# Expert activations and their weighing in one program, with the first weighing group prepared during the last expert steps

## What is computed

```python
best, ci = lax.top_k(cand, 16)            # 16 of 256 candidate pairs, per token and head (8 heads)
e = i1[ci // 16] * 128 + i2[ci % 16]      # expert numbers, 128 picks a token
g = softmax(best)
hid = einsum('td,tkd->tk', xn, u[e])      # one dot product with row e of u
act = gelu(hid) * g
out = einsum('tk,tkd->td', act, v[e])     # weighted sum of rows e of v
```

## Time and profile before

| | us |
|---|---|
| median of three runs (3413.38 to 3416.85) | 3415.7 |
| the profiled execution, its own time | 3419.49 |
| its span in the trace | 3417.7 |
| TensorE busy in the span | 3182.4 (93%) |
| VectorE, ScalarE, GpSimd busy | 2177.6, 1223.9, 1682.6 |

### The profile page before, as it was taken

One profiled execution on the slowest core, in us unless ns is written; L12 is line 12 of the kernel. 1 busy time (PEld: TensorE's weight loads), 2 busy tenths in 40 slices (PEclk: granted clock), 3 DMA queues, 4 the chain that ended last, 5 costly groups with the idle time before them and its releaser, 6 DMA issues. The chain is left out here.

```text
span 3417.7 us, 45006 instructions
## 1 busy us (share of the span) xinstructions
PE 3182.4 (93%) x17090; PEld 2878.5 (84%) x17090; DVE 2177.6 (64%) x3550; ACT 1223.9 (36%) x1895; POOL 1682.6 (49%) x847
## 2 busy tenths in 40 slices
PE   7989678988999999999999999994999999999998
PEld 5777578877889999999999999993888888888886
DVE  2510578824455678687878889773667666666664
ACT  3211347722112225655555656651211211212110
POOL 2411010022203565555554555675878778778783
PEclk9999789999999999999999999997999999999999
DMA  3242652141214676767676767888778788787784
GB/s 136 87 166 76 152 112 47 29 166 59 68 46 133 207 239 193 258 230 240 233 247 222 240 231 233 305 320 326 291 287 308 281 295 291 287 305 274 280 305 149
DMA packets 253406, 713.94 MB, mean 209 GB/s; under 512 B 21681, under 2 KB 79921, under 8 KB 246577
## 3 DMA queue, kind: packets, MB, share of 16 engines
q1 hardware_dynamic: 179504, 443.13, 38.1%
q0 software_dynamic: 73728, 268.47, 22.7%
HBM read 577.31 MB, written 134.22 MB: 208 GB/s over the span
## 5 line engine op out<-in xcount | busy, mean ns | idle before, releaser
L1228 DVE SCALAR_TENSOR_TENSOR found<-found,x_first 128x1024 f32<-128x1024 f32 x232 | 406.5, 1765 | 245.7 <-DMA found<-in_u,pick_u 245.0
L1299 PE MATMUL banks<-side_hi,u_hi 128*128 128x384 f32 x2048 | 533.0, 341 | 14.3 <-issue 14.3
L968 POOL TENSOR_TENSOR u_lo<-u_raw,u_hi 128x1024 fp32r<-128x1024 f32 x127 | 338.8, 2668 | 392.0 <-ACT u_hi L918 391.5
L1299 PE MATMUL banks<-side_lo,u_hi 128*128 128x384 f32 x2048 | 523.7, 336 | 0.0
L1299 PE MATMUL banks<-side_hi,u_lo 128*128 128x384 f32 x2048 | 522.7, 336 | 0.0
L2006 PE MATMUL part<-v_hi,act_hi 128*128 128x512 f32 x1536 | 475.8, 391 | 49.6 <-POOL act_lo L1929 49.6
L2006 PE MATMUL part<-v_lo,act_hi 128*128 128x512 f32 x1536 | 474.7, 390 | 0.0
L2006 PE MATMUL part<-v_hi,act_lo 128*128 128x512 f32 x1536 | 474.2, 390 | 0.0
L977 POOL DMA_INDIRECT found<-in_u,pick_u x232 | 336.6, 1451 | 196.8 <-DVE found L1228 158.8
L1945 DVE TENSOR_TENSOR acc<-acc,part 128x1024 f32<-128x1024 f32 x192 | 234.3, 1220 | 302.6 <-PE part L2006 302.3
L1897 ACT ACTIVATE v_hi<-v_raw 128x2048 fp32r<-128x2048 f32 x64 | 122.9, 1920 | 799.2 <-DMA v_raw<-in_v 614.8
(11 more groups left out here) (217 smaller groups left out, 5196.0 us busy)
## 6 DMA issues: line engine op xcount, KB each, us to landing
u_raw<-in_uT SPq DMA_DIRECT2D x128, 512.0 KB
v_raw<-in_v SPq DMA_DIRECT2D x64, 1024.0 KB
hid_d<-hid SPq DMA_DIRECT2D x128, 384.0 KB, 5.7
gate_d<-stage SPq DMA_DIRECT2D x48, 1024.0 KB
act_in<-hid_d SPq DMA_DIRECT2D x64, 768.0 KB, 7.7
gate_in<-gate_d SPq DMA_DIRECT2D x32, 1536.0 KB
w_raw<-in_w_in SPq DMA_DIRECT2D x6, 2048.0 KB, 8.2
k_hi<-k_hi_d SPq DMA_DIRECT2D x32, 256.0 KB, 8.0
```

Of the source, the lines that this page charges most:

```text
L968: pool.tensor_tensor(u_lo[s % 2][:, :, :], u_raw[:, :, :], u_hi[s % 2][:, :, :].bitcast(F), ALU.subtract).then_inc(u_lo_ok, 1)
L1228: dve.scalar_tensor_tensor(out=found[:, g], in0=found[:, g], scalar=1.0, in1=x_first[:, g], op0=ALU.mult, op1=ALU.mult, accum_out=pick_act ...
L1299: mm = pe.matmul(hid_ps[:, s % 2, half, 0:W], w[s % 2][:, ch], x[:, ch, GB * P + half * W:GB * P + (half + 1) * W], start=n == 0, stop=n = ...
```

## The change

`route`, `hidden` and `weigh` now lie in one program with no barrier between them. The semaphores are made once for all three. `weigh`'s buffers take the place of those of `hidden`, ordered so that what is free early is used early: `v_hi` and `v_lo` are `side_hi` and `side_lo`, the hidden activations of group 0 go to `act_first` and `act_in[1]`, its second pair of `v` to one of the four `found4` buffers.

During the last turn SyncE loads group 0 after step 13 (`load_first`). Group 0's gates are read for 640 of the 768 dense tokens, since the last block's come last (`EARLY_T`). VectorE multiplies after its products of step 15, ScalarE rounds the product ahead of its Gelu of step 15 and `v` behind it. TensorE goes from the last expert step to group 0's item 0. Low parts of group 0's `v` are made by VectorE (columns 0, 1, 3) and GpSimd (column 2). The other 128 tokens follow when the last gates are stored and read back (`last_gates`); item 5 waits for them.

The lags are shorter, `(6, 11)`, and the ranking of blocks 0 and 1 takes fewer slots (`near`), so that gathers begin at steps 6 and 11. In turn 0 there is one product per step and block. `late_picks` then has 6 and 11, over by step 12.

The core of the diff (indentation left out; a line that is only "..." marks what is left out):

```diff
-    LAG = (SLOTS // 2, SLOTS)
+    LAG = m.lag                     # (6, 11)
...
-            return [(g, s * LAG[g] // SLOTS) for g in range(GB) if s * LAG[g] % SLOTS == 0]
+        return [(0, s // 2)] * (s % 2 and s // 2 < LAG[0]) + [(1, s)] * (s < LAG[1])
...
+        def load_first():
+            for n in range(2):
+                sp.wait_ge(hid_out[n], 16 * blocks)
+            sp.wait_ge(stage_out[0], 16 * PARTS * (blocks - GB))
+            sp.wait_ge(stage_out[1], 16 * PARTS * (blocks - GB - 1))
+            for x, rows in ((0, m.act_first), (1, m.act_in[1])):
+                sp.dma_start(rows[:, :, :], hid_d[COLS * x:COLS * x + COLS]...).then_inc(m.a_in[x], 16)
+            sp.dma_start(m.gate_in[:, 0:EARLY_Q], gate_d[0:EARLY_Q, :, 0:2 * COLS]...).then_inc(m.g_in, 16)
+            sp.dma_start(m.v_raw[:, :, :], v_d[0:COLS]...).then_inc(m.v_in, 16)
+            for g in range(GB):
+                sp.wait_ge(late_dotted[g], LAG[g])
+            sp.dma_start(m.found4[1][:, :, :], v_d[COLS:2 * COLS]...).then_inc(m.v_in, 16)
...
+                if last and s == 13:
+                    load_first()
...
-            for n in range(PARTS):
-                store_gates(blocks - 1, PER, n)
-            for s in range(2):
-                sp.wait_ge(hid_out[s], 16 * blocks * SLOTS // 2)
-                sp.wait_ge(stage_out[s], 16 * PARTS * (blocks - GB))
...
-                    if s == (9 if phase and phase <= GB else 12) and not last:
+                if s == (7 if phase == 0 else 9 if phase <= GB else 12) and not last:
                         exponents(tb + 1)
...
+            near = quick and tb < GB
...
-                if phase == 0:
+                if phase == 0 and s == LAG[1] - 1:
                     keep_picks(1)
...
@@ weigh, TensorE: the first group @@
+        def group_first():
+            for n in range(DENSE):
+                if n < BANKS:
+                    pe.wait_ge(m.hid_ok, ALL_STEPS - 1 + n)
+                else:
+                    pe.wait_ge(added, n - BANKS + 1)
+                if n == DENSE - 1:
+                    pe.wait_ge(a_lo_ok, 1 + HALVES)
...
+                    if n == 0:
+                        pe.wait_ge(v_hi_ok, j + 1)
+                        pe.wait_ge(m.a_lo_first if x else a_lo_ok, 1)
...
@@ layer @@
-        weigh(nc, v, hid_d, gate_d, h_d, pick_v, pick_act, out)
+                weigh(nc, block, sem, m, side_hi, side_lo, v, hid_d, gate_d, h_d, pick_v, pick_act, out)
```

More of the change, by code:

```diff
@@ L427, in __init__ @@
[L427 to L436, removed]
@@ L463, in route @@
     KEYS = 2 * PEER_HEADS
[L464 to L524, removed]
@@ new lines, in route @@
+    x_in = sem("x_in3")
+    small_in = sem("small_in3")
+    first_in = [sem(f"first_in3{n}") for n in range(4)]
+    first_lo = [sem("first_lo_pool"), sem("first_lo_dve")]
+    w_in = sem("w_in3")
+    w_hi_ok = sem("w_hi_ok3")
+    w_lo_ok = sem("w_lo_ok3")
+    u_in, u_hi_ok, u_lo_ok = m.u_in, m.u_hi_ok, m.u_lo_ok
+    const_ok = sem("const_ok3")
+    pr_ok = sem("pr_ok3")
+    added = sem("h_added")
+    h_out = sem("h_out")
+    ss_ok = sem("ss_ok3")
+    var_ok = sem("var_ok3")
+    rstd_ok = sem("rstd_ok3")
@@ L775, in hidden @@
+def hidden(nc, block, sem, m, x_hi, x_lo, x_first, iota, iota16, ident, uT_d, u_d, v_d, score_d, hid_d, gate_d,
            pick_v, pick_act, blocks=TB):
@@ new lines, in _, with turn, body @@
+    @block.tensor
+    def _(pe):
+        def turn(tb):
+            pe.wait_ge(looked, LOOKS * (tb + 1))
+            for n, src in enumerate((expert[:, 0], expert[:, 1], share[:, :, :])):
+                last = pe.transpose(turn_ps[:, n], src.rearrange("p h k -> p (h k)"), ident[:, :])
+            last.then_inc(turned, 1)
+        def body(tb, phase, last):
+            for s in range(SLOTS):
+                j = tb * SLOTS + s
+                pe.wait_ge(u_lo_ok, j + 1)
+                if phase == 0 and s < 2:
+                    pe.wait_ge(m.q_ok, 2 * SLOTS)
+                if not (phase == 0 and s < 2):
+                    pe.wait_ge(hid_ok, j - 1)
+                n = 0
+                for ch in range(C):
+                    for w, x in ((u_hi, x_hi), (u_hi, x_lo), (u_lo, x_hi)):
+                        for half in range(2):
+                            mm = pe.matmul(hid_ps[:, s % 2, half, 0:W], w[s % 2][:, ch],
+                                           x[:, ch, GB * P + half * W:GB * P + (half + 1) * W],
+                                           start=n == 0, stop=n == 3 * C - 1)
+                        n += 1
+                mm.then_inc(hid_mm, 1)
+                if s == 15 and phase and not last:
+                    turn(tb + 1)
+                if phase < GB:
+                    continue
+                if not (phase == GB and s == 0):
+                    pe.wait_ge(gate_ok, j - NO_GATES)
+                pe.wait_ge(col_ok, j - NO_GATES + 1)
+                for t in range(TOK):
+                    mm = pe.matmul(gate_ps[:, t], row_hot[:, s % 2, t], col_gate[:, s % 2, t],
+                                   start=True, stop=True)
+                mm.then_inc(gate_mm, 1)
+        for tb in range(GB + 1):
+            body(tb, tb, False)
+        with pe.Fori(GB + 1, blocks - 1) as tb:
+            body(tb, GB + 1, False)
+        body(blocks - 1, GB + 1, True)
```

1887 lines of the change are left out of this document (1028 added, 859 removed), and 3 rows, old and new, of the table EXPERT_SIGNALS.

## The result

| | before | the change |
|---|---|---|
| median of four runs each, us | 3414.5 | 3434.65 (3433.87 to 3435.82) |
| ratio to before | | 1.0061, 95% interval 1.0048 to 1.0074 |
| span of the profiled execution | 3417.7 | 3432.4 |

The account below looks back on a forecast made before the run. The weighing loop was taken as bound by TensorE, the seam costing 55.8 us beyond its own work. Terms left 23.6 us, so 32.2 gained: 3415.7 - 32.2 = 3383.5 us, range 3368 to 3401.

Parts of the forecast that it names:

- The "slower" one: Rival, weighing loop: GpSimd's gathers and low parts settle behind, every group begins with a wait; 3446 us at 2 us each; chance 0.04.
- sign of being wrong: TensorE's waits from 2300 us on not adding up to 14 to 22 us, or waits standing after group 1.
- the late gates: Seam, group 0: last gates read back at 2329, the addition done by 2331.2, in time, so no wait.
- the transfers collide: Rival, seam: loads, stores and gathers share the DMA engines; gain only 18 or 15 us, 3401 us; chance 0.14.
- the lags: Expert steps: gathers beginning at steps 6 and 11 lose nothing and gain nothing, as TensorE had no gap there.
- restart: Start of group 0 at the seam: TensorE idles from 2300.4 to 2307.0, 6.6 us.
- low parts of `v` in item 0: First item of group 0: v blocks follow each 1.06 us, so the item runs through without a wait.
- item 3, the seed: Group 0: the seed's load and copy delay VectorE's second addition to 2326.8; TensorE waits 1.5 us.
- item 5, gates of group 1: Group 0: VectorE waits for group 1's gates before the addition this item needs; TensorE waits 5.9 us.
- group 1, second half: Group 1: GpSimd's low parts are done at 2357.3; TensorE waits 3.6 us from 2353.7.
- lower clock: After seam waits TensorE runs at the lower clock, costing 2.0 us each time.
- The rate of 0.39 MB per us: Seam: the speed at which the full DMA engines were taken to move loads, stores and gathers.

Follow-up runs that it names:

- e1: The change with 32 unused bytes a partition behind its small buffers, moving all buffers of the three stages 32 bytes further on; 3396.4 us, ratio 0.9937.
- e11: The kernel of e1 run again, unchanged, on the chip of e10; 3394.35 us, ratio 0.9938 to the kernel before.
- e7: The kernel of e1 with three of the four last gate stores moved behind the load of group 1's gates; 3408.5 us, ratio 0.9974.
- e8: e7 with the seam reordered: first gate store, seed and late gates ahead of most sums, second v last; 3400.3 us, ratio 0.9956.
- e10: e8 with group 1's v loaded right behind the late gates, its gates last, and ScalarE rounding v without waiting for stores; 3396.7 us, ratio 0.9952.
- e6: The kernel before with only the new lags of 6 and 11 and the earlier ranking of the first two blocks; 3406.9 us, ratio 0.9976.

## Why the prediction was wrong

**The step that failed** is the sentence "New semaphores and unrolled loop turns on SyncE cost nothing visible: under 1 us either way", at the end of its paragraph on the shorter lags. It weighs what the program gained in instructions, and leaves out that joining the programs laid all their buffers out anew. TensorE's time per matmul was taken as a constant of the loop (0.227). It was 0.2338 in the change. That cost 29.9 us in the loop, 1.0 in the 156 matmuls ahead of it (156 x 6.7 ns), 6.7 in `route` (1026.35 less 1019.69 in e1): 37.6 together, and e1 measured 38.2 for the whole. The last term is good to some 3 us: in the kernels whose `route` was fast the first Gelu stood at 1016.9 to 1019.7. None of the rivals had it. The "slower" one (GpSimd's loop settling behind) gave 3446 by another mechanism, of which there is no sign: no wait stands among the 4452 matmuls.

The prediction's own sign of being wrong showed too, apart from the placement: the waits from 2300 on were to be 14 to 22 us, and were 30.4 (29.1 in e11). The largest term behind that is the late gates, put at 0, which measured 7.8.

With the placement mended, e1 and e11 took 3396.4 and 3394.35 us. Those lie inside the range, above the forecast of 3383.5, close to the rival "the transfers collide". In part that is luck: the seam gave 17 us and not 32, and the lags, put at 0, gave 8.4 that the sum didn't have. The rival's terms don't fit one by one either, with 5 us for the seed (measured 0.6) and nothing for the late gates (7.6).

**The seam, term by term** (waits of TensorE in us; the third clock term falls behind the seam as measured here):

| term | predicted | change | e11 |
|---|---|---|---|
| restart | 6.6 | 8.2 | 8.0 |
| low parts of `v` in item 0 | 0 | 1.4 | 1.1 |
| item 3, the seed | 1.5 | 0.5 | 0.6 |
| item 4, the late gates | 0 | 7.8 | 7.6 |
| item 5, gates of group 1 | 5.9 | 6.7 | 6.1 |
| group 1, second half | 3.6 | 5.8 | 5.7 |
| lower clock | 4.0 | 5.8 | 7.5 |

The last row is what is left of the seam: 72.7 - 30.4 - 156 x 0.2338 for the change, 72.0 - 29.1 - 156 x 0.2271 for e11. Predicted were 21.6 us, measured 36.2 and 36.6: the gain is 17 us, where 32.2 stood.

- *Restart*: right in kind and near in size. VectorE's last product ended 2.3 us behind the last expert matmul (2303.02 + 1.22), where 0.5 was said; the chain has its gather at 10.59 us, where 5.1 to 8.9 had been read. The v blocks followed as foreseen.
- *The late gates* are the term of the seam that was mis-sized most. The prediction has "the rest of 0.79" MB behind the first store, which is three quarters of 1.05: four stores taken as 1.05 MB in all. Each is 1 MB. The first landed 14.5 us after its issue and the reading back took another 11.6: at 2342.78, where 2329 was said. Counted from the last expert matmul that is 40.9 us for 28.6. The first store alone landed 4.7 later than said (29.3 for 24.6), and e7 shows the part of the 3.1 MB behind it: 7.5 us. VectorE stood behind it:

```profile
2342.78 0.42 DVE L2090 TENSOR_TENSOR act_first<-act_first,gate_in 128x256 f32<-128x256 f32 x1 [11.45 <-DMA gate_in<-gate_d]
...
2353.45 1.76 DVE L2082 TENSOR_TENSOR act_in<-act_in,gate_in 128x1536 f32<-128x1536 f32 x1 [8.78 <-DMA gate_in<-gate_d]
```

  and so did the addition for item 4, which was expected "in time". That the queue of VectorE decides, not the transfer alone, was right.
- *Item 5 and group 1* came in the foreseen places by the foreseen engines, 0.8 and 2.2 us longer.
- *The rate of 0.39 MB per us* was right. The windows of the change from 2310 to 2340 show it:

```profile
2310.00:2320.00 10.00, 8.51 (x28) 6.12 (x29) 9.81 (x9) 5.16 (x6) 2.68 (x1) 0.81 1.00 377
2320.00:2330.00 10.00, 10.00 (x45) 8.03 (x44) 3.01 (x3) 0.00 (x0) 3.77 (x4) 1.00 1.00 386
2330.00:2340.00 10.00, 6.40 (x27) 4.51 (x25) 1.33 (x2) 0.00 (x0) 0.00 (x0) 1.00 1.02 423
```

  The 341 GB/s for transfers of 1 MB that the Trainium skill gives ("DMA: Bandwidth & Descriptors", Bandwidth) would be too low here. Its other rule that the prediction weighed (the Trainium skill, the same page, Issuing engines are not separate DMA queues: all of them share the same 16 engines) agrees with the gather of GpSimd that took 10.59 us from 2292.41 on, beside SyncE's loads. What is put ahead in SyncE's own queue also pushed something else back in e8 (`v(1,0)`) and e10 (the gates of group 1).
- *After group 1* no wait stands, as said.

**The lags** were put at 0, by the argument that TensorE had no gap in the first steps. That was so, and no wait for picks came in turn 0; but e6 is 8.4 us shorter than before. The gain lies behind them: turns 0 and 1 (16 steps each, from Gelu to Gelu) take 133.2 and 133.5 us in every profile, and the differences stand in the later turns and in the first wait of the seam.

## What to carry to other kernels

When a change moves buffers, by merging programs or adding even a few bytes ahead of them, compare the addresses of every matmul's two operands before and after, not only the instructions; a full TensorE at full clock that does fewer matmuls per microsecond points there, and a pad that brings their distance back to what it was, modulo 256 bytes (32 bytes here), tells whether it is so. Add up the bytes of a seam from the shapes of each transfer: where the DMA engines are full, another order of the queue mostly moved the wait here, and three tries gained nothing. Fewer bytes or an earlier start weren't tried. And time each part of a composite change on its own: here one part (the lags) gave 8 us, one (the seam) some 13 to 15, and one that nobody had meant took 38.

## What the hardware did that was not expected

- A matmul of 512 fp32r columns costs 0.227 us where weights and streamed operand are a multiple of 256 bytes apart in SBUF, and 0.2334 to 0.2338 where they are 32, 64, 128 or 224 bytes off that; between these distances there is no slope. Both times are above what the Trainium skill ("TensorE: Matmul & The Clock Gate", Back-to-back issue gap) works out for one alone, 512/2.4 + 2.5 = 216 ns. Why 384 columns don't show it (0.1735 us at either distance) is open. So is whether the distance within the two buffers matters: all offsets used here, 512 bytes per block of weights and 2048 per half row of `v`, are multiples of 256 themselves.
- The granted clock falls to its lower level several times in the expert steps, at different places in each execution. Together with TensorE's short waits this sets the spread of the experts' time: 44 us of both in e1 (34.2 + 10.2, experts 1277.9) and 37 in e8 (25.5 + 11.9, experts 1269.8). e1 and e11 are the same kernel and differ by 4.7 us there (1277.9 and 1273.2). What makes the waits come and go from one execution to the next is open.
